# Six feed-forward stages multiply x times the norm's weights in every gate and up pair, and VectorE applies rstd behind the products

## What is computed

```python
def rmsnorm(x, g):
    xf = x.astype(jnp.float32)
    y = xf * lax.rsqrt(jnp.mean(xf * xf, axis=-1, keepdims=True) + EPS)
    return (y * g.astype(jnp.float32)).astype(x.dtype)
def swiglu(h, w_gate, w_up, w_down):
    return (jax.nn.silu(h @ w_gate) * (h @ w_up)) @ w_down
...
    x = x + 0.5 * swiglu(rmsnorm(x, ffn1_norm), ffn1_wg, ffn1_wu, ffn1_wd)
    h = rmsnorm(x, mix_norm)
...
    x = x + 0.5 * swiglu(rmsnorm(x, ffn2_norm), ffn2_wg, ffn2_wu, ffn2_wd)
```

## Time and profile before

| | |
|---|---|
| median of 3 runs | 2116.55 us (2115.03 to 2117.78) |
| the profiled execution | 2120.99 us, of which the span of the profile is 2119.0 us |
| PE busy, PE weight loads | 97%, 86% of the span |
| DVE, ACT, POOL busy | 75%, 57%, 2% |
| mean granted clock of PE | 0.982 of full speed |
| HBM read | 423.8 MB, 200 GB/s over the span |
| PE's instructions | 13033 matmuls, 13040 weight loads |

### The profile page before, as it was taken

The page is one execution under the profiler, slowest core; times in us unless marked ns, Lnnn a source line. Parts: engine busy times, 40 slices in busy tenths (PEclk is TensorE's granted clock), DMA queues, the critical chain, the costliest instruction groups (busy, mean ns, idle before and its releaser), DMA issues.

```text
span 2119.0 us, 32267 instructions
## 1 busy us (share of the span) xinstructions
PE 2059.0 (97%) x13033; PEld 1812.2 (86%) x13040; DVE 1594.4 (75%) x2540; ACT 1213.3 (57%) x2095; POOL 39.8 (2%) x39
## 2 busy tenths in 40 slices
PE   8999999999999999999899998899999999899998
PEld 7889898888888899888788897888888889668887
DVE  7887677887888766888678876688876667668664
ACT  6555666555555566655465556665565545446553
POOL 0002000000001100000000000000000000000000
PEclk9999999999999999999999999999999999899999
DMA  7877334876687532587658753368755455104543
GB/s 269 311 269 246 127 113 162 295 263 218 233 283 265 209 137 100 206 290 254 203 205 288 243 193 123 104 245 286 236 200 193 162 203 179 60 21 169 188 169 129
DMA packets 78090, 426.53 MB, mean 201 GB/s; under 512 B 9696, under 2 KB 10592, under 8 KB 47632
## 3 DMA queue, kind: packets, MB, share of 16 engines
q1 hardware_dynamic: 77968, 424.88, 57.9%
HBM read 423.80 MB, written 1.05 MB: 200 GB/s over the span
## 4 chain that ended last, share of the span: by engine, by line
PE 80%; DVE 11%; DMA 4%; ACT 3%; issue 2%; POOL 0%; DVEq 0%; ACTq 0%; POOLq 0%
PE bank L494 39%; PE bank L498 20%; DVE slot_lo L1490 4%; PE bank L476 3%; PE bank L477 3%; PE bank L478 3%; DMA slot<-in_wd_dram 2%; ACT slot_hi L1074 1%; PE bank L724 1%; DMA slot<-in_slots_dram 1%; PE bank L486 1%; DVE h L1542 1%; PE bank L544 1%; PE bank L545 1%; PE bank L546 1%
## 5 line engine op out<-in xcount | busy, mean ns | idle before, releaser
L1490 DVE TENSOR_TENSOR slot_lo<-slot,slot_hi 128x1024 fp32r<-128x1024 f32 (+1 forms) x728 | 801.4, 1115 | 189.7 <-ACT slot_hi L1074 188.7
L1074 ACT ACTIVATE slot_hi<-slot 128x1024 fp32r<-128x1024 f32 (+1 forms) x728 | 679.1, 957 | 229.4 <-PE bank L494 94.7
L494 PE MATMUL bank<-h_both,slot_hi 128*128 128x512 f32 x2592 | 650.3, 392 | 0.0
L494 PEld LDWEIGHTS bank<-h_both,slot_hi 128*128 128x128 f32 x2592 | 466.2, 189 | 83.0
L498 PEld LDWEIGHTS bank<-h_both,slot_lo 128*128 128x128 f32 x2592 | 353.6, 190 | 25.3
L498 PE MATMUL bank<-h_both,slot_lo 128*128 128x256 f32 x2592 | 361.4, 282 | 0.0
L494 PE MATMUL bank<-act_both,slot_hi 128*128 128x512 f32 x1232 | 307.1, 395 | 0.0
L1148 ACT ACTIVATE room<-bank 128x512 f32<-128x512 f32 x170 | 101.5, 597 | 303.2 <-PE bank L494 303.2
L494 PEld LDWEIGHTS bank<-act_both,slot_hi 128*128 128x128 f32 x1232 | 223.7, 188 | 46.0
L476 PE MATMUL bank<-h_both,slot_hi 128*128 128x256 f32 x720 | 213.7, 297 | 6.9 <-ACT h L1346 3.1
L1646 DVE TENSOR_TENSOR room<-room,bank 128x512 f32<-128x512 f32 x170 | 116.7, 686 | 126.8 <-ACT room L1148 126.6
(11 more groups left out here) (276 smaller groups left out, 2202.9 us busy)
## 6 DMA issues: line engine op xcount, KB each, us to landing
slot<-in_slots_dram SPq DMA_DIRECT2D x236, 1024.0 KB, 4.8
slot<-in_wd_dram SPq DMA_DIRECT2D x128, 704.0 KB, 4.1
room<-in_mod_w_dram SPq DMA_DIRECT2D x144, 512.0 KB, 4.9
room<-in_na_bias_dram SPq DMA_DIRECT2D x8, 512.0 KB, 6.1
x<-in_x_dram SPq DMA_DIRECT2D x1, 1024.0 KB, 4.8
out_dram<-h SPq DMA_DIRECT2D x4, 256.0 KB, 2.2
cond<-in_cond_dram SPq DMA_DIRECT2D x1, 512.0 KB, 9.4
room<-in_gla_mask_dram SPq DMA_DIRECT2D x1, 512.0 KB, 5.6
```

The costliest lines, as they stand in the source:

```text
L494: return pe.matmul(o, slot_hi[b][:, w:w + P], x_both.rearrange("p a b -> p (a b)"), start=first, stop=last)
L1074: act.activation(slot_hi[b][:, c0:c1], slot[raw][:, c0:c1], ACT.Copy).then_inc(s["hi_ready"], 1)
L1490: ins = dve.tensor_tensor(slot_lo[b][:, c0:c1], slot[raw][:, c0:c1], slot_hi[b][:, c0:c1].bitcast(F32), ALU.subtract)
```

## The change

In the six stages, all 22 pairs are multiplied with u instead of h, each with `three` (`gate_up_scaled`), unit by unit and chunk by chunk. ACT's copy of the low half and DVE's addition go; instead DVE multiplies each pair from PSUM by rstd (L1660 now), and in the second stack copies that pair's shift column to `pair_shift` first. The normalised h is not made any more in these stages: DVE's 16 and ACT's 8 instructions at the stage's start go, and what remains there is `rstd_behind`. Since u must live through all pairs, it stands in `u_room`, the former `second_u`, at the end of `room`, where neither `act_both` nor the modulation buffers lie. `scaled_x` gives `h_both` in stage (0,1,0). The stages (0,0,0) and (1,0,0) keep the old way, so six stages change; the words that came with the change say seven.

```diff
--- before.py
+++ after.py
@@ -192,10 +192,8 @@
         ROOM = 19008
         U_COLS = S + 2
         U_PLACE = ROOM - 2 * KC * U_COLS
-        with nc.sbuf_tensor("first_u", [P, KC, 2, U_COLS], F32R) as first_u:
-            pass
         with nc.sbuf_tensor("below_u", [P, U_PLACE], F32):
-            with nc.sbuf_tensor("second_u", [P, KC, 2, U_COLS], F32R) as second_u:
+            with nc.sbuf_tensor("u_room", [P, KC, 2, U_COLS], F32R) as u_room:
                 pass
         room = sb("room", [P, ROOM])
 
@@ -264,12 +262,11 @@
         q_rope = carve(at, 4, 512)
 
         first_shift = sb("first_shift", [P, 2])
+        pair_shift = sb("pair_shift", [P, 2, 2])
 
         def scaled_x(stack, mixer_done):
 
-            if mixer_done:
-                return first_u
-            return second_u if stack else h_both
+            return u_room if stack or mixer_done else h_both
 
         def gain_of(stack, layer, i, k):
             return mod_gain[:, layer, i, k:k + 1] if stack else gains[:, 3 * layer + i, k:k + 1]
@@ -558,7 +555,7 @@
                     for unit in range(2):
                         last = three(targets[unit][:, 0:cols], (unit * KC + k) * P, u[:, k, 0, 0:cols], u[:, k, 1, 0:cols], b,
                                      k == 0 and (unit == 0 or targets[2]), k == KC - 1, True)
-                    if i < 2 and stack == 0 and k < KC - 1:
+                    if i == 1 and stack == 0 and k < KC - 1:
                         last.then_inc(s["u_read"], 1)
                 last.then_inc(s["slot_done"], 1)
 
@@ -583,15 +580,30 @@
 
                 nonlocal used
 
-                def gate_up(c, fresh=None):
+                def gate_up_normalised(c, fresh=None):
                     pe.wait_ge(s["pair_read"], seen("pair_read"))
                     pair_products(next_slot(), c % 2, fresh)
 
+                def gate_up_scaled(c, first=False):
+                    pe.wait_ge(s["pair_read"], seen("pair_read"))
+                    if first:
+                        first_products(stack, i, (pair_bank[0][:, 0, :], pair_bank[0][:, 1, :], True))
+                        return
+                    b, u = next_slot(), scaled_x(stack, i == 2)
+                    cols = U_COLS if stack else S
+                    pe.wait_ge(s["lo_ready"], seen("lo_ready"))
+                    for unit in range(2):
+                        for k in range(KC):
+                            last = three(pair_bank[c % 2][:, unit, 0:cols], (unit * KC + k) * P, u[:, k, 0, 0:cols], u[:, k, 1, 0:cols],
+                                         b, k == 0, k == KC - 1)
+                    last.then_inc(s["slot_done"], 1)
+
                 if hidden_norm(layer, i):
-                    pe.wait_ge(s["pair_read"], seen("pair_read"))
-                    first_products(stack, i, (pair_bank[0][:, 0, :], pair_bank[0][:, 1, :], True))
-                    gate_up(1, "h_ready")
+                    gate_up = gate_up_scaled
+                    gate_up(0, True)
+                    gate_up(1)
                 else:
+                    gate_up = gate_up_normalised
                     gate_up(0, "h_ready")
                     gate_up(1)
                 turns = (FC - 2) // (2 * SPLIT_RING)
@@ -1106,11 +1118,14 @@
                     ins.then_inc(s["h_hi_ready"], 1)
                 split_hi()
 
-            def hidden(shift=None, read=False):
+            def rstd_behind():
 
                 split_hi_half(0)
                 rstd_of(rstd[:, :], bank[4][:, 0:S], D)
                 split_hi_half(1)
+
+            def hidden(shift=None, read=False):
+                rstd_behind()
                 for k in range(KC):
                     act.wait_ge(s["h_raw"], seen("h_raw"))
                     if read and k < KC - 1:
@@ -1134,7 +1149,7 @@
             def ffn(stack, layer, i, last_one=False):
                 first = hidden_norm(layer, i)
                 if first:
-                    hidden(shift_of(stack, layer, i), stack == 0 and i == 0)
+                    rstd_behind()
                 else:
                     norm(shift_of(stack, layer, i))
                 if stack == layer == i == 0:
@@ -1144,11 +1159,11 @@
                 def gate(c):
                     b = c % 2
                     act.wait_ge(s["slot_done"], seen("slot_done"))
-                    if c or not first:
+                    if not first:
                         act.activation(gate_up_f[:, b, :, :], pair_bank[b][:, :, S:2 * S], ACT.Copy).then_inc(s["pair_half"], 1)
                     split_hi_half(0)
                     act.wait_ge(s["pair_read"], seen("pair_read"))
-                    bias = first_shift[:, 0:1] if first and stack and c == 0 else 0.0
+                    bias = pair_shift[:, b, 0:1] if first and stack else 0.0
                     act.activation(gate_up_f[:, b, 0, :], gate_up_f[:, b, 0, :], ACT.Silu, bias=bias).then_inc(s["sil_ready"], 1)
                     split_hi_half(1)
                     act.wait_ge(s["act_raw"], seen("act_raw"))
@@ -1619,16 +1634,13 @@
 
             def ffn(stack, layer, i, last_one=False):
                 done = seen.value("slot_done")
-
-                def first():
-                    dve.wait_ge(s["slot_done"], done + 1)
-                    if stack:
-                        dve.tensor_copy(first_shift[:, :].unsqueeze(2), pair_bank[0][:, :, S:S + 1])
-                    dve.tensor_tensor(gate_up_f[:, 0, :, :], pair_bank[0][:, :, 0:S], both(rstd[:, :]), ALU.mult
-                                      ).then_inc(s["pair_read"], 1)
-
                 hidden_first = hidden_norm(layer, i)
-                norm_of(stack, layer, i, first if hidden_first else None)
+                if hidden_first:
+                    split_lo(0)
+                    dve.wait_ge(s["rstd_ready"], seen("rstd_ready"))
+                    split_lo(1)
+                else:
+                    norm_of(stack, layer, i)
                 group = (stack * LAYERS + layer) * 2 + i // 2
                 modulation = group < MOD_GROUPS
                 if group == 0:
@@ -1641,14 +1653,20 @@
 
                 def hidden(c, b):
 
-                    if c or not hidden_first:
+                    if hidden_first:
+                        dve.wait_ge(s["slot_done"], done + c + 1)
+                        if stack:
+                            dve.tensor_copy(pair_shift[:, b, :].unsqueeze(2), pair_bank[b][:, :, S:S + 1])
+                        dve.tensor_tensor(gate_up_f[:, b, :, :], pair_bank[b][:, :, 0:S], both(rstd[:, :]), ALU.mult
+                                          ).then_inc(s["pair_read"], 1)
+                    else:
                         dve.wait_ge(s["pair_half"], seen("pair_half"))
                         dve.tensor_tensor(gate_up_f[:, b, :, :], gate_up_f[:, b, :, :], pair_bank[b][:, :, 0:S], ALU.add
                                           ).then_inc(s["pair_read"], 1)
                     split_lo(0)
                     dve.wait_ge(s["sil_ready"], seen("sil_ready"))
-                    if c == 0 and hidden_first and stack:
-                        dve.scalar_tensor_tensor(out=act_f[:, b, :], in0=gate_up_f[:, b, 1, :], scalar=first_shift[:, 1:2],
+                    if hidden_first and stack:
+                        dve.scalar_tensor_tensor(out=act_f[:, b, :], in0=gate_up_f[:, b, 1, :], scalar=pair_shift[:, b, 1:2],
                                                  in1=gate_up_f[:, b, 0, :], op0=ALU.add, op1=ALU.mult).then_inc(s["act_raw"], 1)
                     else:
                         dve.tensor_tensor(act_f[:, b, :], gate_up_f[:, b, 0, :], gate_up_f[:, b, 1, :], ALU.mult
```

## The result

| | before | after |
|---|---|---|
| median, lowest to highest | 2115.79 us (2114.07 to 2119.09), 6 runs | 2126.07 us (2125.39 to 2129.84), 6 runs |
| profiled execution, span | 2120.99 us, 2119.0 us | 2129.84 us, 2128.1 us |

The ratio is 1.0044, with an interval of 1.0033 to 1.0055: the kernel became slower by 10.3 us, where 13.3 were forecast. It is slower for the reason that was given; one term of the sum was too large (22.3 us where the trace has 17.4).

The account below looks back on a forecast made before the run. The prediction took PE, busy for 97% of the span, as the bound. It summed +22.3 - 7.5 - 1.5 = +13.3 us, added to the median of 2116.55 us for 2129.9 us, 0.6% slower, with a range of 2123 to 2137 us.

Parts of the forecast that it names:

- PE is the bound and pays in full: Inside a stage: PE busy 97%, so ACT's and DVE's savings are worth nothing there and PE's extra work costs fully.
- The price of a pair: 20 pairs in each of six stages: 5.76 or 5.78 us instead of 5.584, together +22.3 us.
- The lower bound of the forecast: Narrow matmuls at 0.119 us each, 5.71 us a pair: +15.4 us over 120 pairs, 2123 us in all.
- Pair 1: Start of the six stages: no more wait for h, 34.6 us instead of 42.1, so -7.5 us.
- nothing is won in (0,1,0): Pair 1 of that stage: PE was late for other reasons, so h was ready and no wait is saved.
- The second down slot: End of the gate and up pairs: the wait for the last act_lo goes, 6 x 0.25 = -1.5 us.
- Narrow matmuls are cheap: Same 120 pairs: under 5.66 us a pair the kernel is faster, 2100 us at 5.52; chance of faster 0.04.
- The loop body doesn't stay: Jumps back in the six-pair loop: the longer body may wait for instruction loads, 2134 to 2156 us; chance 0.06.
- DVE becomes the bound: Four stages with modulation: DVE's chain at 5.9 us a pair would cost 11 us more, 2141 us; chance 0.04.
- Its cover: DVE in stages with modulation: done 5.26 us after the pair, 0.5 us before the next at 5.76.

Follow-up runs that it names:

- e3: The kernel before, with pairs 1 to 21 of the six stages as three narrow matmuls on normalised h, without ACT's copy: 2137.48 us, ratio 1.0082.
- e8: The kernel before with h_both moved by 32 bytes and everything behind it by 96: 2111.38 us, ratio 0.9965.
- e9: The kernel before with h_both in place and everything behind it 64 bytes further up: 2117.35 us, ratio 0.9998.
- e4: The kernel before with pair 1 of the six stages also on u, pairs 2 to 21 wide on h: 2109.73 us, ratio 0.9956.
- e5: The changed kernel with h_both moved by 32 bytes and everything behind it by 96: 2114.34 us, ratio 0.9986 to the kernel before.
- e12: The kernel of e4 with h_both and everything behind it 64 bytes further up: 2095.59 us, ratio 0.9900 to the kernel before.

## Why the prediction was right, and where it was off

**PE is the bound and pays in full: right.** Removing 78 us of ACT's work and 26 of DVE's moved nothing between the pairs; e3 shows the price alone.

**The price of a pair: mis-sized.** This is the term that was too large, by 4.9 us: "A pair of 256 columns then takes 16 x 0.360 = 5.76 us", from the earlier trace rows, and 5.78 for 258 columns. The rows were read rightly, but the operand of those with 256 columns lies in `h_both`, and of the six stages only (0,1,0) has its u there: 40 x 0.07 = 2.8 us of the 4.9. The rows with 258 columns are nine steps in `first_u`, at 0.361 us for three; over whole pairs in `u_room` it is 0.359, which gives 60 x 0.033 = 2.0 us. The duration of one does not tell the two places apart. L475's matmuls in the change, pair 0 and 1 of (0,0,2) and the start of (0,1,0), with 282 and 283 ns in the median:

```profile
L475 PE MATMUL bank<-u_room,slot_lo x34: 274/282/286, 341.0 to 355.7; 128*128 128x256 f32 x34
...
L475 PE MATMUL bank<-h_both,slot_lo x33: 278/283/416, 531.9 to 548.7; 128*128 128x256 f32 x33
```

The steps from start to start do: in `h_both` they are 0.120 us each; in `u_room` they vary between 0.112 and 0.124 with a mean of 5.693 / 48 = 0.1186, and with 258 columns the mean is 0.1197 us. The term then is 40 x 0.105 + 20 x 0.17 + 60 x 0.163 = 4.2 + 3.4 + 9.8 = **+17.4 us** in place of 22.3. The lower bound of the forecast, 0.119 us a matmul, was not low enough for the first stack's place. With 48 x 20 = 960 such matmuls in each of six stages, 0.001 us a matmul is 5.8 us.

**Pair 1: right.** 5.70, 5.76, 5.69, 5.75, 5.74 and 5.74 us, together 34.4 (forecast 34.6): -7.7 us, forecast -7.5. e3 kept the narrow form and the h, and kept the waits. One reading of the prediction does not hold in general: that nothing is won in (0,1,0), whose pair 1 took 5.68 us. That was so in this profiled execution: its granted clock was 0.74 from 531.1 to 540.0 us, PE took 12.35 us from the last down product to the start of pair 1, and h was ready. In e8, the kernel before but moved, the clock was 1.00 in that stretch, and PE took 10.04 us. The last matmul of pair 0 there and the first of pair 2:

```profile
539.14 0.27 PE L480 MATMUL bank<-h_both,slot_lo 128*128 128x256 f32 x1
...
546.23 0.39 PE L496 MATMUL bank<-h_both,slot_hi 128*128 128x512 f32 x1
```

Less 0.12, that is 6.97 us for pair 1 (6.90 in e9, 6.93 in e3). So where the clock is not cut there, the change, and e4 too, saves about 1.3 us more than was counted.

**The second down slot: right**, 6 x 0.25 = -1.5 us, by the rows above.

**Sum.** 17.4 - 7.7 - 1.5 = +8.2 us, against +9.1 us of span and +10.3 us (7.0 to 11.6 by the ratio's interval) of time. The last microsecond lies between the stages, where PE waits and its granted clock falls at other moments (0.74 of full speed from 531.1 to 540.0 us before and 0.82 after, but 1.00 and 0.72 from 733 to 739 us); it wasn't followed further.

**The rivals.** *Narrow matmuls are cheap* fell for this kernel: it needed a pair under 5.66 us in all six stages. But it was nearer than its 0.04 said. At other places the narrow form is at 5.60 us, and the wide one moves too, so even there the change costs about 4.5 us (e5 against e8). *The loop body doesn't stay:* there is no gap behind a sixth pair, and from 353 to 460 us, around the loop of (0,0,2), q8 moved two packets before and two after (a second such queue, q14, which the earlier trace rows show and the prediction passed over, also two and two). The price is 0. Of the Trainium skill's two statements ("Runtime: NRT & Kernel Launch", section Instruction fetch mechanics) the one that gives PE 128 KiB fits this; a refetch at a jump out of a window of two pages is not seen with a body of 576 instructions. *DVE becomes the bound:* it did not. 84 us of (0,0,2) after, in the view of windows (PE, PEld, DVE, ACT, POOL, clock, DMA share, GB/s):

```profile
362.90:446.70 83.80, 83.80 (x709) 83.80 (x708) 71.81 (x105) 39.44 (x59) 0.00 (x0) 1.00 0.78 268
```

DVE is busy for 71.8 of 83.8 us (73.6 before), and PE for all of them. Its cover of about 0.5 us a pair held: DVE waited 0.42 us for PE at each pair with a modulation product, and 1.57 us at those without.

The Trainium skill's gap of N / 2.4 + 2.5 ns ("TensorE: Matmul & The Clock Gate", section Back-to-back issue gap), which the page gives for an isolated matmul, would be 109 ns for 256 columns, by an estimate. The lowest mean that any run here showed, with own weights each time, is 5.60 / 48 = 0.1167 us, so the trace's price stays the one to use.

## What to carry to other kernels

When an engine is the bound, count its instructions first; work taken from the others is worth only the waits that it ends. So take the saving where the waits are and keep the cheap form elsewhere: one pair on u (e4) gained 9.3 us, all 21 of them lost 10.3. Price each form from rows with the same operand at the same place, and when the bound is matmuls, try the hot buffers at a few starts 32 bytes apart: 64 bytes of padding were worth 11.9 us (e12 against e4), about as much as the rewrite moved. Read the starts from the allocator, not from the padding that was asked for.

## What the runs showed of the hardware that was not expected

The step of the same matmul (128x128 fp32r weights of its own, 256 moving columns, granted clock 1.00) was 0.120, 0.1167, 0.1178 and 0.1183 us with the moving operand (`h_both` or u, rows of 1024 bytes) starting 0, 32, 64 and 96 bytes past a multiple of 128, up to 2.8%. In `act_both` it was 0.1187, 0.1178 and 0.120 us at 32, 64 and 96, so the offset alone does not say it. A pair with wide matmuls of 512 columns has another order: 5.59, 5.60 and 5.51 us at 0, 32 and 64. Over this kernel, moving buffers alone changed the time by 0.35% (e8), and moving everything behind `h_both` by 64 bytes by nothing that could be measured (e9, 0.9998, from 0.9986 to 1.0011).
